# The low part of every odd weight chunk made by GpSimd instead of VectorE, in a two-block fp32 model on one core

## What is computed

```
h = x + gla_mixer(rmsnorm(x)) @ ...          # w_in 2048 x 6160, w_out 2048 x 2048
h = h + relu(rmsnorm(h) @ w_up)**2 @ w_down  # 2048 x 8192 and 8192 x 2048
h = rmsnorm(h)
h = h + concat(attention, rg_lru)(rmsnorm(h) @ w_in_2) @ w_out_2   # 2048 x 6144, 2048 x 2048
```

## Time and profile before

| | before |
|---|---|
| median of the runs | 1519.02 us |
| span of the profiled execution | 1514.3 us |
| TensorE (PE) busy | 1497.6 us, 99% |
| VectorE (DVE) busy | 843.5 us, 56% |
| ScalarE (ACT) busy | 711.9 us, 47% |
| GpSimd (POOL) busy | 30.8 us, 2% |
| mean DMA rate | 183 GB/s |
| granted TensorE clock | 1.000 of full speed |

### The profile page before, as it was taken

How to read it: one execution, slowest core, us unless ns; L and a number is a source line. 1 busy time by engine, 2 the same in 40 slices (tenths; PEclk the granted TensorE clock), 3 DMA queues, 4 the chain that set the end, 5 groups by cost and what they waited for, 6 DMA issues and landing times. The chain is left out here.

```text
span 1514.3 us, 19184 instructions
## 1 busy us (share of the span) xinstructions
PE 1497.6 (99%) x6826; PEld 1237.1 (82%) x6826; DVE 843.5 (56%) x872; ACT 711.9 (47%) x856; POOL 30.8 (2%) x54
## 2 busy tenths in 40 slices
PE   7999999999999999999999999999999999999998
PEld 6788888888888888888888888888888888888886
DVE  5555545555555545555555554555566776565653
ACT  5544544445444433443344433444654664565532
POOL 3000000000000000000000000000000011000000
PEclk9999999999999999999999999999999999999999
DMA  8455565657666666666666666666556566545564
GB/s 267 137 167 154 145 202 176 187 176 240 192 183 182 192 192 194 185 182 188 194 189 184 189 190 191 189 190 185 182 180 181 154 194 191 166 144 167 181 193 140
DMA packets 144721, 277.03 MB, mean 183 GB/s; under 512 B 10800, under 2 KB 10912, under 8 KB 144512
## 3 DMA queue, kind: packets, MB, share of 16 engines
q1 hardware_dynamic: 143056, 271.75, 59.3%
q0 software_dynamic: 1040, 3.07, 0.6%
q10 hardware_dynamic: 544, 1.05, 0.2%
HBM read 273.74 MB, written 2.10 MB: 182 GB/s over the span
## 5 line engine op out<-in xcount | busy, mean ns | idle before, releaser
L1003 DVE TENSOR_TENSOR w_lo<-raw,w_hi 128x1024 fp32r<-128x1024 f32 x508 | 620.2, 1225 | 610.7 <-ACT w_hi L706 609.3
L706 ACT ACTIVATE w_hi<-raw 128x1024 fp32r<-128x1024 f32 x508 | 537.0, 1059 | 731.7 <-PE acc L420 710.5
L418 PE MATMUL acc<-w_hi,xa_hi 128*128 128x512 f32 x1276 | 506.3, 397 | 1.6 <-issue 1.4
L420 PE MATMUL acc<-w_hi,xa_lo 128*128 128x512 f32 x1276 | 497.3, 390 | 0.0
L419 PE MATMUL acc<-w_lo,xa_hi 128*128 128x512 f32 x1276 | 496.7, 389 | 0.0
L418 PE MATMUL acc<-w_hi,xb_hi 128*128 128x512 f32 x768 | 300.1, 391 | 1.5 <-DVE w_lo L1003 1.5
L420 PE MATMUL acc<-w_hi,xb_lo 128*128 128x512 f32 x768 | 299.0, 389 | 0.0
L419 PE MATMUL acc<-w_lo,xb_hi 128*128 128x512 f32 x768 | 298.8, 389 | 0.0
L418 PEld LDWEIGHTS acc<-w_hi,xa_hi 128*128 128x128 f32 x1276 | 239.7, 188 | 52.0 <-issue 3.2
L420 PEld LDWEIGHTS acc<-w_hi,xa_lo 128*128 128x128 f32 x1276 | 239.5, 188 | 50.7
L419 PEld LDWEIGHTS acc<-w_lo,xa_hi 128*128 128x128 f32 x1276 | 239.9, 188 | 49.4 <-issue 1.9
(11 more groups left out here) (198 smaller groups left out, 513.1 us busy)
## 6 DMA issues: line engine op xcount, KB each, us to landing
raw<-in_mlp_w_up SPq DMA_DIRECT2D x128, 512.0 KB, 3.7
raw<-in_mlp_w_down SPq DMA_DIRECT2D x128, 512.0 KB, 4.4
raw<-in_gla_w_in SPq DMA_DIRECT2D x96, 512.0 KB, 3.8
raw<-in_w_in SPq DMA_DIRECT2D x96, 512.0 KB, 3.7
raw<-in_gla_w_out SPq DMA_DIRECT2D x32, 512.0 KB, 4.5
raw<-in_w_out SPq DMA_DIRECT2D x32, 512.0 KB, 4.7
result<-stage SPq DMA_DIRECT2D x8, 256.0 KB, 3.3
h<-in_x ACTq DMA_DIRECT2D x2, 512.0 KB, 6.4
```

The source lines that it names most:

```text
L418: pe.matmul(o, xh[:, kt, xs], w_hi[:, n % RING, k, :], start=kt == 0, stop=False)
L420: last = pe.matmul(o, xl[:, kt, xs], w_hi[:, n % RING, k, :], start=False, stop=kt == KT - 1)
L706: act.activation(w_hi[:, n % RING, :, :], raw[:, n % RING, :, :], ACT.Copy)\
L1003: dve.tensor_tensor(w_lo[:, n % RING, :, :], raw[:, n % RING, :, :], w_hi[:, n % RING, :, :].bitcast(F32), ALU.subtract).then_inc(lo_ready, 1)
```

## The change

For every chunk n of 4 or more with n odd, the subtraction is issued by GpSimd (`sum_lo`) and not by VectorE; even chunks and the first four stay with VectorE. Since the ring has four buffers, odd chunks are always buffers 1 and 3. GpSimd counts a new semaphore, `lo_pool`; `lo_ready` now counts VectorE's chunks alone. TensorE waits for the one or the other by the chunk's parity, and so does the load of chunk n+4 on SyncE's queue. GpSimd's program becomes a list by steps (t, c) as the other engines have: the powers and the three late DMAs, which before stood one after the other, now stand between subtractions.

```
+def lows(n):
+    return n // 2 + 1 + sum(i % 2 for i in range(min(n + 1, RING)))
+def pool_lows(n):
+    return (n - RING) // 2 + 1
...
             def load(c, n0, it, per, src):
                 n = n0 + c
-                if it is None:
-                    if n >= RING:
-                        sp.wait_ge(lo_ready, n - RING + 1)
-                elif n >= RING:
-                    sp.wait_ge(lo_ready, it * per + (n - RING + 1))
+                m = n - RING
+                if m >= RING and m % 2:
+                    had = pool_lows(m)
+                    sp.wait_ge(lo_pool, had if it is None else it * (per // 2) + had)
+                elif m >= 0:
+                    had = lows(m)
+                    sp.wait_ge(lo_ready, had if it is None else it * (per // 2) + had)
...
+            def sum_lo(t, c, it):
+                n = CH * t + RING + c
+                if n >= CH * PANELS or c % 2 == 0:
+                    return
+                pool.wait_ge(hi_ready, at(lambda q: CH * q + RING + c + 1, t, it))
+                pool.tensor_tensor(w_lo[:, n % RING, :, :], raw[:, n % RING, :, :],
+                                   w_hi[:, n % RING, :, :].bitcast(F32), ALU.subtract).then_inc(lo_pool, 1)
+            def run(t, it=None):
+                for c in range(CH):
+                    prev = KINDS[t - 1] if t else ""
+                    if (t, c) == (0, 7):
+                        power(ST_X)
+                    if prev == "v" and c == 4:
+                        power(ST_O + (t - 5) // 2)
+                    if (t, c) == (FIRST_U, 2):
+                        power(ST_MLP)
+                    if (t, c) == (FIRST_X, 4):
+                        power(ST_FIN)
+                    if (t, c) == (FIRST_X, 6):
+                        power(ST_N2)
+                    if prev and prev in "KQ" and c == 2:
+                        power(ST_KQ + t - 1 - 50)
...
+                    sum_lo(t, c, it)
...
-                pe.wait_ge(lo_ready, at(lambda q: CH * q + c + 1, t, it))
+                if n >= RING and c % 2:
+                    pe.wait_ge(lo_pool, at(lambda q: pool_lows(CH * q + c), t, it))
+                else:
+                    pe.wait_ge(lo_ready, at(lambda q: lows(CH * q + c), t, it))
...
             def split_lo(t, c, it):
                 n = CH * t + RING + c
-                if n >= CH * PANELS:
+                if n >= CH * PANELS or c % 2:
                     return
```

More of the change, by code:

```diff
@@ L190, in gated_block_kernel @@
         hi_ready, lo_ready = sem("hi_ready"), sem("lo_ready")
+        lo_pool = sem("lo_pool")
         chunk_used = sem("chunk_used")
@@ L375, in _ @@
             pool.wait_ge(consts, 3)
[L376 to L384, removed]
+            def sum_lo(t, c, it):
[20 more added lines that the diff above has]
+                        power(ST_KQ + t - 1 - 50)
+                    if (t, c) == (FIRST_O + 1, 2):
+                        pool.wait_ge(chunk_used, CH * (FIRST_O + 1))
+                        pool.wait_ge(tp_lo, groups_before(FIRST_O + 1))
+                        pool.dma_start(fin_gain, final_norm.partition_broadcast(P)).then_inc(late_in, 16)
+                        pool.dma_start(lru_w[:, 0, :, :], lru_w_a_2[0].rearrange("g i j -> i g j")).then_inc(late_in, 16)
+                        pool.dma_start(lru_w[:, 1, :, :], lru_w_x_2[0].rearrange("g i j -> i g j")).then_inc(late_in, 16)
+                    sum_lo(t, c, it)
+            for t in range(PANELS):
+                run(t)
         @block.tensor
```

## The result

The changed kernel takes **1526.94 us** (median of two runs, 1526.62 and 1527.27) against 1519.02, so it is 7.9 us slower. The record gives the ratio as 1.0062, with a 95% interval of 1.0045 to 1.0078; the quotient of these two medians is 1.0052, which lies within it. The loss is clear of the interval and about a quarter of the 2% (30 us) from which the forecast speaks of a change. Its profiled execution has a span of 1525.4 us and a device time of 1527.27, so 1.9 us lie around the span.

What follows compares the result with a forecast made beforehand. TensorE was taken to bound the kernel, busy 1497.6 us of a 1514.3 us span. 1514.3 - 0.4 + 1.3 + 1.2 = 1516.4 us of span, plus 4.7, gave 1521 us; range 1516 to 1532.

Steps and rivals of the forecast that it cites:

- the likeliest case: Whole kernel: subtractions hidden, small costs only; 1521 us, own range 1517 to 1526, chance 0.76.
- third rival: Convolution to end of scans: 20 odd chunks add 24 us of shared port, half comes through; 1533 us, chance 0.12.
- Rivals 2 and 4: 2: VectorE relieved, no holding, 1517.5 us, chance 0.07. 4: GpSimd becomes the bound at every odd chunk, chance 0.05.
- GpSimd's subtraction, 2.4 us: Each odd chunk's subtraction on GpSimd, estimated from fills and a small cast: 2.4 us, ends 0.95 and 4.7.
- VectorE's busy time, 532 us: Whole kernel: VectorE's busy time falls from 843.5 by 312 us to near 532 us.
- Steady stretches, 0: Steady stretches: GpSimd's rate and the four-buffer ring hide its subtraction, so it costs nothing.
- The start, -0.4: At the start TensorE's wait of 1.01 us for `xa_lo` shrinks: gain 0.4 us, between 0 and 1.01.
- The spot in panels 50 and 51, +1.3: Ahead of chunk 412, GpSimd's chunk 411 holds VectorE between scans: +1.3 us, ends -0.2 and +3.7.
- Everything else in the dense stretch, 0: Powers between subtractions and later reads of `rs` cost 0; TensorE stands at only one spot there.
- The end, +1.2: Chunk 507's subtraction grows from 1.24 to 2.4 us and shifts the last chain: +1.2 us, ends -0.3 and +3.5.
- The threshold of rival 4, 5.44 us of GpSimd's work: Every odd chunk: GpSimd becomes the bound once a subtraction with its hold-ups takes over 5.44 us.
- The 4.7 us between span and median: Whole kernel: median of runs minus profiled span, 1519.0 - 1514.3 = 4.7 us, added to the predicted span.

Runs made afterwards that it cites:

- experiment 2: Changed kernel with the odd chunks 401 to 423 (12 of 254, panels 49 to 51) given back to VectorE: 1518.74 us, ratio 1.0008.
- experiment 5: Changed kernel with GpSimd casting `raw` into `w_lo` of the odd chunks (one operand read) instead of subtracting: 1517.01 us, ratio 1.0001.
- experiment 4: Changed kernel with GpSimd filling `w_lo` of the odd chunks for about 2.4 us, reading nothing, their low parts left out: 1517.18 us, ratio 0.9998.
- Experiment 9: Kernel before the change, with GpSimd subtracting only chunks 5 and 508: 1515.17 us, ratio 0.9985.
- experiment 1: The changed kernel once more, no edit, in more rounds: 1525.99 us, ratio 1.0055.
- experiment 6: Changed kernel with each of GpSimd's 254 subtractions made twice, same result: 1651.77 us, ratio 1.0893.
- experiment 3: Kernel before, all subtractions on VectorE, plus GpSimd subtractions of constants that nobody waits for, once per odd chunk in panels 17 to 51: 1531.99 us, ratio 1.0095.
- experiment 8: Changed kernel with GpSimd subtracting the even chunks from 4 on instead of the odd ones: 1533.12 us, ratio 1.0112.
- experiment 10: Kernel before the change, with GpSimd subtracting chunk 508 alone: 1515.61 us, ratio 0.9986.

## Why the prediction was right or wrong

**The time and its class: right, the mechanism only in part.** 1526.9 lies inside 1516 to 1532 and within 2%, but 0.9 us above the likeliest case's own range. What happened is my third rival, the contended port in the busy stretch, to which I gave 0.12, at a little over half its price: 1533 was 14 us above before, and it became 7.9, of which 7.25 hang on that stretch (experiment 2). The sum had a change of 2 us and four times that came; that the range held it is owed to the share of rival 3 that I had let in. Rivals 2 and 4 did not come true.

**GpSimd's subtraction, 2.4 us: the right number by wrong working.** It takes 2.40 undisturbed, 2.419 in the mean. I had taken 0.71 ns for each element read from a cast of 128x128, fixed cost and all. The cast of 1024 elements takes 1.06 us (experiment 5), so one read adds only 0.11 us to the fill's 0.95; the second operand adds 1.34. GpSimd's busy time came to 644.7 for 640.

The prediction also says that 2.25 us would make the sum 0.15 us shorter; the figure stands in two terms (+1.3 and +1.2), so it would be 0.3.

**VectorE's busy time, 532 us: missed, 616.9.** I said that two-operand instructions would be lengthened, and did not add it up. Of the 85 us about 76 are lengthened instructions, holding that the trace books as busy time; the rest is that instructions overlapped their neighbours by more before. Of these 16 x 1.66 = 26.6 us are the squarings, and they cost nothing: with them still held in experiment 2 the time is within a microsecond or so of before's. The page "SBUF — State Buffer" of the Trainium skill (section "SBUF: two separate sides") has VectorE with two operands in SBUF blocked only against a GpSimd operation that reads SBUF; experiments 4 and 5 agree, 481 ns a tap beside fills and 570 beside a cast. It says too that a VectorE operation in a 2-port mode is blocked by any; the casts of 530 ns beside fills would fit, but no run shows in which mode a cast runs.

**Steady stretches, 0: right.** Between 790 and 1172 us of before the lag of the same matmuls stays at 1.4 us.

**The start, -0.4: near.** TensorE waits 0.85 for 1.01, a gain of 0.16. Experiment 9 bears out that nothing more is to be had there.

**The spot in panels 50 and 51, +1.3: near, by a wrong reading.** The wait for chunk 412 went from 0.18 to 1.61, within the 1 to 2 us of the forecast's signs, and one of 0.19 for chunk 410 is new; the lag grows by 1.9 at the two. But I had let go the holding by chunk 409, because the even chunk behind it would wait for a cast ending at 1197.61. That is the cast of chunk 411; chunk 410's had ended at 1195.42, and what kept its subtraction until 1197.74 was the four taps ahead of it. GpSimd could so begin 409 and 411 at the taps and not at the scans, and both held a tap there (5.88 us for 1.7). My upper end, +3.7, reckoned with both.

**Everything else in the dense stretch, 0: the step that failed.** "TensorE stands at only one spot there now" left out all the others, and they cost 7.0 of the 8.9 us; experiment 2 puts 7.25 us of time on the twelve chunks of the whole stretch. First, the taps of panel 49 were off the chain of before. Once they took 9.4 us for 5.1, their end came 2.30 us too late for TensorE (1176.67), and with the restart and 3.4 us at half clock that cost 4.2. I had looked for who is late, not for who becomes late when VectorE's dense blocks grow by 4 us. Second, the taps at 1214.87 were held once more (3.81 for 1.67), and chunk 414 behind them came 0.42 late: 0.7 us. Third, I had set the powers and `rs` at 0: the scaling by `rs` was held 2.2 us, and the transposes behind it waited 1.87, which cost 2.1.

**The end, +1.2: half.** The link grew by the 1.17 that I had worked out; the DMA behind it landed 0.6 sooner than before's, so the wait grew by 0.6, and by 0.3 in experiment 1. I had taken one landing (5.84) for fixed.

**The threshold of rival 4, 5.44 us of GpSimd's work: wrong.** At 4.8 us the loss was already 134 us (experiment 6). The two engines' time on the port adds up; the threshold is about 5.44 less VectorE's 0.9 to 1.2 in the same two chunks; this is worked out from experiment 6's rounds, and no run between 2.4 and 4.8 us tries it.

**The 4.7 us between span and median: wrong as an offset.** In the changed kernel and the experiments the device time is 1.7 to 2.3 us above the span of the same execution. The profiled execution of before was a quick one; the other 2.6 us or so are spread between executions. This error was luck: it is opposite to that of the sum, and with an offset of 2.1 the forecast would have been 1518.5, further from the result.

**What stays open.** In seven profiles (the changed kernel and experiments 1, 2, 3, 5, 6 and 9) the granted clock falls for some 3 us near 73 us. Busy time by stretch, first the changed kernel, then the kernel before:

```profile
72.10:75.40 3.30, 3.30 (x9) 2.60 (x8) 0.00 (x0) 0.93 (x2) 2.37 (x1) 0.51 0.02 6
```
```profile
72.10:75.40 3.30, 3.30 (x14) 2.44 (x13) 1.89 (x2) 2.15 (x4) 0.00 (x0) 1.00 0.03 11
```

TensorE is listed as busy without a gap before it, unlike at 1176, but what it does there is small. Changed kernel:

```profile
67.62 3.63 PE L542 MATMUL aux<-spans,arena 128*128 128x7 f32 x32
```

The kernel before runs the same 32 matmuls of seven columns in the same 3.63 us (line 501) with no dip behind them, so they alone do not decide it. The dip costs 1.6 us here, up to 3.2 in experiments 5 and 9. It comes in experiments 3 and 9, whose GpSimd does nothing new at that time, and not in experiments 4, 8 and 10, so it is not shown to come from the change; its cause is not settled. Two waits at the ends of loops, near 610 and 789 us, vary from 0.2 to 1.5 between the kernels, and no run here tells what sets them.

## What to carry to other kernels

Treat GpSimd's reading instructions and VectorE's instructions with two operands in SBUF as users of one resource: add their times per period against the period, and again in each stretch where VectorE is dense, and follow every instruction behind a held one to who waits for it. An engine that is half idle is no reason to move its work when the engine that is the bound doesn't wait for it. Move the single instruction that stands behind a blocked queue (here one of 508, which gave 0.14%), not every second one.

## What the runs showed of the hardware that I had not expected

- A held VectorE instruction shows as a longer one, with no idle time before it: 2.5 us and more for 480 ns (a mean of 921 over 24 taps, five of them held), 2887 ns for 1225. The mean of an instruction form in two traces shows contention where the list of waits shows none.
- Instructions with one operand are held too, and even by fills, which read nothing. In experiment 4, VectorE's time line and GpSimd's:

```profile
1227.83 0.69 DVE L1086 TENSOR_SCALAR ms<-sums 128x8 f32<-128x8 f32 x1
```
```profile
1227.55 0.95 POOL L405 MEMSET w_lo<- 128x1024 f32 x1 [4.94 <-ACT w_hi L758]
```

  It takes 0.17 us alone, and here it ends as the fill does (1228.50). Beside a subtraction it takes up to 2.23. A VectorE addition with one operand in PSUM and one in SBUF (line 1147, 1221 ns in the changed kernel) was not lengthened, though seven of the 20 fell beside a subtraction.
- GpSimd's second operand costs 1.34 us for 1024 elements and the first 0.11: cast 1.06, fill 0.95, subtraction 2.40.
- GpSimd is held in turn: 3.26 us for 2.40.
- TensorE's granted clock was 0.50 (the 1.2 GHz level) for 3.4 us, beginning 1.4 us after a wait of 2.30 us had ended, and in experiment 4 again for 3.4 us, from 1499.4 to 1502.8, about 1 us after a wait of 1.83. A wait can so cost more than its length. It need not: behind the wait of 2.07 at the end of the changed kernel the clock stayed at 1.00.
